# GpSimd's order of gathers in a mixer and expert layer: V row k+4 before U row k in the second group, U row 4 before U row 3 in the first

## What is computed

```python
def peer_ffn(xn, w_query, sub_keys, expert_u, expert_v):
    ...
    def block(xb):
        ...
        top_s, pos = lax.top_k(cand, PEER_TOPK)
        idx = jnp.take_along_axis(cidx, pos, axis=-1)
        g = jax.nn.softmax(top_s, axis=-1)
        a = jax.nn.gelu(jnp.einsum('thkd,td->thk', expert_u[idx], xb).astype(jnp.float32))
        return jnp.einsum('thk,thkd->td', (g * a).astype(xb.dtype), expert_v[idx])
```

## Time and profile before

| | us |
|---|---|
| Time, median of 3 runs | 1854.15 (1852.88 to 1854.96) |
| The profiled execution, its own time | 1858.54 |
| its span, first to last instruction | 1856.7 |
| TensorE busy | 1565.3 (84%) |
| VectorE busy | 1097.8 (59%) |
| GpSimd busy | 842.4 (45%) |
| ScalarE busy | 406.3 (22%) |
| Matrix bytes by GpSimd's queue | 542.41 MB, 70.6% of 16 engines' span |

### The profile page before, as it was taken

How to read it: one execution, slowest core, us unless ns; L and a number is a source line. 1 busy time by engine, 2 the same in 40 slices (tenths; PEclk the granted TensorE clock), 3 DMA queues, 4 the chain that set the end, 5 groups by cost and what they waited for, 6 DMA issues and landing times.

```text
span 1856.7 us, 16305 instructions
## 1 busy us (share of the span) xinstructions
PE 1565.3 (84%) x5478; PEld 922.6 (50%) x5478; DVE 1097.8 (59%) x1526; ACT 406.3 (22%) x586; POOL 842.4 (45%) x1091
## 2 busy tenths in 40 slices
PE   8999999999987989987777767777777777877897
PEld 8998888789643444443322223222222223323486
DVE  6667645556766555656555555655556665554755
ACT  4435445332111010110111011011101101111254
POOL 1000000002666666756666756666666656566400
PEclk9999999999988999999999999999999999999999
DMA  7445535767999999999999999999999999999952
GB/s 256 159 147 171 180 120 177 276 218 277 411 405 415 421 419 422 420 421 418 421 422 421 421 422 421 422 422 422 422 422 423 422 422 421 422 405 422 389 195 78
DMA packets 130630, 648.38 MB, mean 349 GB/s; under 512 B 14156, under 2 KB 14264, under 8 KB 64264
## 3 DMA queue, kind: packets, MB, share of 16 engines
q0 software_dynamic: 74640, 542.41, 70.6%
q1 hardware_dynamic: 55728, 105.09, 16.7%
q10 hardware_dynamic: 200, 0.06, 0.0%
HBM read 645.42 MB, written 2.10 MB: 349 GB/s over the span
## 4 chain that ended last, share of the span: by engine, by line
PE 31%; POOL 31%; issue 19%; DMA 15%; DVE 2%; ACT 1%; POOLq 0%; DVEq 0%; ACTq 0%; SPq 0%
PE acc L1595 16%; DMA v_ring<-in_peer_v_dram,idxv 13%; POOL v_ring L490 9%; POOL u_ring L483 9%; POOL tick L489 8%; PE acc L1626 4%; POOL tick L482 3%; DMA u_ring<-in_peer_u_dram,idxu 2%; PE mix L1595 2%; PE acc L1914 2%; PE mix L1914 2%; PE acc L1812 1%; POOL u_ring L496 1%; PE mix L1669 1%; PE acc L1612 1%
## 5 line engine op out<-in xcount | busy, mean ns | idle before, releaser
L1364 DVE CUSTOM_DVE_ANT_0 u_ring<-u_ring,xn 128x2048 f32<-128x2048 f32 x256 | 586.9, 2293 | 463.8 <-DMA u_ring<-in_peer_u_dram,idxu 462.5
L1914 PE MATMUL mix<-v_ring,diag 128*128 128x512 f32 x1024 | 484.3, 618 | 128.4 <-DMA v_ring<-in_peer_v_dram,idxv 115.7
L1914 PE MATMUL acc<-v_ring,diag 128*128 128x512 f32 x960 | 440.9, 603 | 140.2 <-DMA v_ring<-in_peer_v_dram,idxv 136.9
L1914 PEld LDWEIGHTS mix<-v_ring,diag 128*128 128x128 f32 x1024 | 192.0, 196 | 389.9 <-issue 251.0
L1914 PEld LDWEIGHTS acc<-v_ring,diag 128*128 128x128 f32 x960 | 174.0, 190 | 405.0 <-issue 221.9
L489 POOL TENSOR_TENSOR tick<-tick 128x1 f32<-128x1 f32 x224 | 197.7, 882 | 298.8 <-PE acc L1914 153.5
L816 ACT ACTIVATE diag<-ident,wgt 128x128 f32<-128x128 f32 x224 | 86.0, 398 | 766.4 <-PE mix L1914 385.4
L483 POOL DMA_INDIRECT u_ring<-in_peer_u_dram,idxu x224 | 225.6, 1007 | 35.4 <-issue 31.9
L490 POOL DMA_INDIRECT v_ring<-in_peer_v_dram,idxv x224 | 224.2, 1001 | 35.0 <-issue 6.8
L971 DVE TENSOR_TENSOR w_lo<-raw,w_hi 128x2048 fp32r<-128x2048 f32 x63 | 144.4, 2292 | 141.5 <-ACT w_hi L600 140.3
L600 ACT ACTIVATE w_hi<-raw 128x2048 fp32r<-128x2048 f32 x64 | 122.4, 1914 | 206.6 <-PE acc L1595 149.3
(11 more groups left out here) (335 smaller groups left out, 1534.0 us busy)
## 6 DMA issues: line engine op xcount, KB each, us to landing
raw<-in_w_in_dram SPq DMA_DIRECT2D x48, 1024.0 KB, 5.2
raw<-in_w_out_dram SPq DMA_DIRECT2D x16, 1024.0 KB, 5.6
raw<-in_w_ple_gate_dram SPq DMA_DIRECT2D x16, 1024.0 KB, 5.7
raw<-in_peer_query_dram SPq DMA_DIRECT2D x5, 1024.0 KB, 5.1
qw_u<-in_peer_query_dram SPq DMA_DIRECT2D x4, 1024.0 KB, 15.2
qw_v<-in_peer_query_dram SPq DMA_DIRECT2D x4, 1024.0 KB, 9.1
u_ring<-in_peer_u_dram,idxu POOLq DMA_INDIRECT x256
v_ring<-in_peer_v_dram,idxv POOLq DMA_INDIRECT x248, 14.9
```

The costliest lines, as they stand in the source:

```text
L1364: V.tensor_tensor_reduce(out=u_ring[:, k % DEEP, :], in0=u_ring[:, k % DEEP, :], in1=xn2[:, b, :], scale=1.0, scalar=0.0, op0=ALU.mult, op ...
L1914: ins = T.matmul(pairs[j // 2][:, (j % 2) * CW:(j % 2 + 1) * CW], diag[:, k % DEEP, :], v_ring[:, k % DEEP, j * CW:(j + 1) * CW], start=Fa ...
```

## The change

On GpSimd, in the first group, U row 4 is issued before U row 3, and VectorE's products of the first group follow the same order (0, 1, 2, 4, 3, 5, ...). The waits on `u_free` in the first group are counted by the place of a product in this order, so U row 7, which takes row 3's slot, waits for the fifth product. In the second group V row k+4 is issued before U row k, from k = 0 on; before, V row k+3 stood behind U row k, from k = 1 on.

```diff
+        first_order = [0, 1, 2, 4, 3] + list(range(5, TOPK))
...
+                def first_row_u(k):
+                    if k >= DEEP:
+                        pool.wait_ge(u_free, DEEP + first_order.index(k - DEEP) + 1)
+                    elif k < DEEP - 1:
+                        pool.wait_ge(u_slot_read, k + 1)
+                    else:
+                        pool.wait_ge(q_ready, 2)
+                    nc.gpsimd.indirect_dma_start(
+                        u_ring[:, k % DEEP, :], None, u_rows,
+                        bass.IndirectOffsetOnAxis(idxu[:, 0, k:k + 1], 0)).then_inc(u_in[k % DEEP], 16)
...
-                    for k in range(AHEAD):
-                        if k < DEEP - 1:
-                            pool.wait_ge(u_slot_read, k + 1)
-                        if k == DEEP - 1:
-                            pool.wait_ge(q_ready, 2)
-                        row_u(0, 0, k)
+                    for k in first_order[:AHEAD]:
+                        first_row_u(k)
...
                     for k in range(TOPK):
+                        if k < TOPK - DEEP:
+                            row_v(0, 1, k + DEEP)
                         row_u(1, 1, k)
-                        if 1 <= k < 1 + TOPK - DEEP:
-                            row_v(0, 1, k + DEEP - 1)
...
-                for k in range(TOPK):
+                for n, k in enumerate(first_order):
                     products(0, 0, (k,))
-                    if k == FIRST:
+                    if n == FIRST:
                         first_weights()
-                    if k < STAGES // 2:
-                        top_k_stage(1, STAGES // 2 + k)
+                    if n < STAGES // 2:
+                        top_k_stage(1, STAGES // 2 + n)
```

More of the change, by code:

```diff
@@ L525, in first_group @@
                         row_v(0, 1, k)
-                        row_u(0, 0, AHEAD + 2 * k)
-                        row_u(0, 0, AHEAD + 2 * k + 1)
+                        first_row_u(AHEAD + 2 * k)
+                        first_row_u(AHEAD + 2 * k + 1)
                 def second_group():
```

## The result

The changed kernel takes 1863.3 us (median of 5 runs, 1861.23 to 1866.98), the kernel before 1854.15 us; the ratio is 1.0051 with a 95% interval of 1.0039 to 1.0062. It is 0.51% slower, some 9 us; +7.4 us and 1861.5 us were forecast, with a range of 1854.0 to 1864.5 that holds the median.

What follows compares the result with a forecast made beforehand. The prediction took the stream of gathers, one row every 2.49 us, to bound the kernel. It summed 2.5 - 0.5 + 5.4 = +7.4 us on the 1854.15 us median to 1861.5 us, range 1854.0 to 1864.5.

Steps and rivals of the forecast that it cites:

- The bound: From 465 to about 1760 us a chain of gathers, one landing every 2.49 us; time changes only where the stream runs dry.
- Row 4 before row 3: First group: row 4 is held by product 1 as row 3 was, so the rows only change places; gain 0.
- Row 7: First group: row 7's gather, waiting for the fifth product, is held 3.02 us by the sixth; the stream runs dry, +2.5 us.
- the forecast's case: Row 2's landing on an empty queue: issue ended 456.94, product began 461.42; less VectorE's 0.05, taken as 4.4 us.
- The upper bound of 4.4 us: First group: row 7's delay becomes +4.4 us if the row behind pays the thin queue once more.
- Rival 2: First group: row 7's gather wins its race with the sixth product; sum +5.4 us, 1859.5 us; chance 0.10.
- The thin stretch: Second group, 512 to 525 us at 360 GB/s: V rows issued ahead close it, -0.5 us by landings.
- the 1.9 us by bytes: Other end of the gain at 512 to 525 us: 13 x (1 - 360/421) = 1.9 us.
- The second hole: End of second group: five U rows in a row delay GpSimd's small operations and the third group's first gather; +5.4 us.
- row 15 landing at the same place: End of second group: assumed row 15 lands as before, so products 11 to 15 start 2.49 us apart, 568.8 to 578.7.
- The sum: 2.5 - 0.5 + 5.4 = +7.4 us, put on the median of 1854.15 us: 1861.5 us, +0.39%.
- The release of a held gather: A gather held by a VectorE product ends 0.81 us after it by the trace; the Trainium skill says about 115 ns.

Runs made afterwards that it cites:

- p1_race: p1 with one 1.3 us top-k stage on VectorE moved from before the fifth product to behind it; ratio 0.9999 to the kernel before.
- p1_lose: p1 with the short top-k stage behind the fifth product moved ahead of it, so the sixth starts directly after; ratio 1.0019 to the kernel before.
- p1: Changed kernel with the second group put back as before, only the first group's reordering kept; 1858.71 us, ratio 1.0024 to the kernel before.
- p2: Changed kernel with the first group put back as before, only the second group's V row k+4 before U row k kept; 1859.76 us, ratio 1.0029.
- v15_back: The whole change, but V row 15 of the second group issued behind U row 12, not ahead of U row 11; 1860.55 us, ratio 1.0033.
- p2_copy_early: p2 with the V index copy for the third group done at the second group's start, and one addition fewer; 1857.36 us, ratio 1.0019.

## Why the prediction was right, step by step

**The bound.** Right: 421 GB/s in both kernels from 600 to 1640 us, and a delay before that reaches the end. The table shows 1.2 us less delay at group 5 than in group 3 (+9.9 there, +8.7 here), but all eleven traces lose 0.5 to 1.8 us between these two places, so most of it belongs to the one trace of before and not to the change.

**Row 4 before row 3.** Right to the hundredth: held to 456.70, no gain. Overlooked: the index copy behind the two rows is now held by product 2 (L526, 2.32 us), which makes row 5's issue 0.6 us late, and the product of row 4 starts 0.3 us late (462.61 here, which is 466.15 in before's time, against 465.85), though its gather ended on time.

**Row 7.** The mechanism is right, and p1_race and p1_lose show it. It was forecast as held for 3.02 us and was held for 3.02. The size was low: 2.5 us forecast, 3.1 at row 7 and 3.9 at row 8. Of the 0.6 us at row 7 half was there already, since the fifth product itself was 0.3 us late. The rest is the landing on an empty queue: 4.7 us from the issue's end to the product (472.00 to 476.70), where the forecast's case had 4.5 (456.94 to 461.42). Then the row behind pays again: 476.70 to 482.49 is 5.8 us, where a V row and a U row take 4.98. The upper bound of 4.4 us was there for that second payment, and 3.9 is near it. Rival 2, that GpSimd wins, was not wrong either: in p1's profiled execution it did. It was given a chance of 0.10; of the three traces with this code it won one.

**The thin stretch.** Right: 422 GB/s there, and by U row 5 of group 1, the forecast's own place, the gain is 0.5 us: two more V rows (4.98 us) stand ahead of it, and it is only 4.46 later (+3.70 to +8.16). By row 14 it is 1.1 us (+3.7 to +2.6), in p2 1.2 (-0.7 to -1.9); the 1.9 us by bytes are not reached. The column of row 15 of group 1 in the table shows less of it, because that row is already late by the second hole.

**The second hole.** The mechanism is right: v15_back takes away the stretch without a byte (and leaves 2.6 us of delay), and p2_copy_early shortens the hole. The size was low again: 5.4 us forecast and 6.8 measured, from row 14 of group 1 (+2.6) to row 15 of group 2 (+9.4); 7.0 in p2. The step that didn't hold is "row 15 landing at the same place": its gather was held, and its product came 0.7 us late. The first gather of the third group was out only behind product 15, as forecast, but not because the small operations took until then: they were done at 578.33, and the gather itself began 0.14 behind product 15 and was held to 581.64. In before's time (3.54 us more, less the shift of 2.6) that is 582.6, where the forecast said 582.2. The landing took 4.9 us (581.64 to 586.55). By the first product of the third group the hole is 5.4 us (+2.6 to +8.0), the forecast's number, but that is luck in part: the gather's and the landing's extra 0.8 us are offset by the place it was counted from: the forecast put it at 581.2, and before's own product starts at 582.09, since VectorE worked on the weights of the second group until 581.93. The row behind paid again (592.61 less 586.55 is 6.1 us, where two rows take 4.98).

**The sum.** By the trace, 3.7 (row 15 of group 0) - 1.1 + 6.8 (to row 15 of group 2) - 1.1 (to group 15) = 8.3 us against the 7.4 forecast; the medians give 9.1, with 7.2 to 11.5 by the interval of the ratio. The forecast's middle values left out that the row behind an empty queue pays too, at both holes, and that row 15 would be held. Its reason for the 4.4 us between before's profiled execution and its median, that the profiled one carries the profiler, is wrong: the change's profiled execution took 1863.3 us, its median. Before's was a late one: its first index tile is 2.9 to 4.9 us behind that of all other traces. To put the sum on the median was right all the same.

**The release of a held gather.** Row 7 in the change: product 468.90 + 2.29 = 471.19, gather's end 472.00, 0.81 later as in the earlier trace rows. The Trainium skill ("SBUF — State Buffer", the two sides of SBUF) gives about 115 ns; the measurement decides for 0.81. Small operations are out much sooner: the additions of 573.48 and 575.37 end 0.04 and 0.05 us after the products that held them (572.83 and 575.30).

## What to carry to other kernels

Where one queue of gathers bounds a kernel, the order of issue matters only through the times at which that queue is empty, and these are set by what the issuing engine is held by. Before rows of one kind are bunched, look at what else the issuing engine has to do beside them, and leave the busy engine a gap there. A wait that ends with the same event as the other engine's next instruction is a race, whose loser pays for a whole instruction; one short operation moved between them fixes the winner.

## What the runs showed of the hardware

- After a gather on an empty queue the product that waits for it starts 4.5 to 4.9 us after the issue's end (456.94 to 461.42 in before, 472.00 to 476.70 and 581.64 to 586.55 in the change, 470.80 to 475.50 in p1_lose), where a full queue gives one row every 2.49 us. The next U row behind the gap is late by another 0.8 to 1.1 us.
- A gather of GpSimd that starts 0.02 us ahead of a product takes 0.94 us; one that starts 0.08 behind takes 3.02. In eight of the traces (before, the change, p1, p2, p1_race, p1_lose, v15_back, p2_copy_early), from 450 to 1760 us, all 255 gathers that began 0.05 us or more after the start of a product, and while it ran, ended 0.80 to 0.87 us after it. The three that began 0.02 or 0.03 behind were not held.
- Small operations on GpSimd (one column) that are held in this way end about 0.05 us after the product.
